# Attention values one unit later, and five input and two memory weight chunks in products of rounded parts, in a fused transformer kernel on one Trainium2 core

## The reference

```python
h = _rmsnorm(x, norm_mix[l])
proj = h @ w_in[l]
(c_q, c_kv, k_rope, fq, fk, fv, f_logit, cq, ck, cv) = jnp.split(proj, IN_SPLIT_POINTS, axis=-1)
ya = _mla(c_q, c_kv, k_rope, ...)      # 4 heads, q and kv from low-rank latents
yb = _fox(fq, fk, fv, f_logit, ...)    # 4 heads, scores with a cumulative forget term
yc = _chunk_rel(cq, ck, cv, ...)       # 4 heads, banded, relative bias
...
k, v = jnp.split(m @ w_ckv, 2, axis=-1)   # _cross: keys and values of the normed memory
...
p = jax.nn.softmax(sc, axis=-1)
return jnp.einsum('bhqk,bkhd->bqhd', p, v)
```

## Time and profile before

| | |
|---|---|
| median of 3 runs | 2479.87 us (2477.61 to 2480.54) |
| the profiled execution | 2479.72 us |
| its span, first to last instruction | 2477.9 us |
| mean granted TensorE clock | 0.989 of full speed |
| TensorE busy, weight loads busy | 96%, 84% of the span |
| VectorE, ScalarE, GpSimd busy | 77%, 21%, 12% |
| start up to the first attention's scores | 0 to 102.0 us |
| first attention (scores to last values) | 102.0 to 157.1 us |
| second attention | 213.9 to 229.4 us |
| third attention | 1503.1 to 1548.2 us |

### The profile page before, as it was taken

How to read it: one execution, slowest core, us unless ns; L and a number is a source line. 1 busy time by engine, 2 the same in 40 slices (tenths; PEclk the granted TensorE clock), 3 DMA queues, 4 the chain that set the end, 5 groups by cost and what they waited for, 6 DMA issues and landing times.

```text
span 2477.9 us, 38599 instructions
## 1 busy us (share of the span) xinstructions
PE 2387.2 (96%) x14244; PEld 2069.3 (84%) x14244; DVE 1908.7 (77%) x3950; ACT 530.2 (21%) x956; POOL 298.0 (12%) x228
## 2 busy tenths in 40 slices
PE   8998999999999999999999997899999999999998
PEld 7765998669897899999999876598978999999997
DVE  2226787768998788888888775489987888888887
ACT  2324333222233200000000145222332000000001
POOL 0000000016581000000000000165810000000000
PEclk9989999999999999999999999999999999999999
DMA  6504688963314555555555551133145555555553
GB/s 223 192 32 166 244 315 324 363 256 129 102 52 145 179 185 187 186 186 186 186 186 186 189 201 50 68 136 101 46 150 173 186 186 186 186 186 186 186 186 127
DMA packets 97875, 430.07 MB, mean 174 GB/s; under 512 B 11249, under 2 KB 11889, under 8 KB 90865
## 3 DMA queue, kind: packets, MB, share of 16 engines
q1 hardware_dynamic: 97776, 428.75, 48.6%
HBM read 427.66 MB, written 1.05 MB: 173 GB/s over the span
## 4 chain that ended last, share of the span: by engine, by line
PE 84%; DVE 12%; ACT 2%; issue 1%; DMA 1%; SPq 0%; DVEq 0%; ACTq 0%; PEldq 0%
PE ps L497 64%; PE ps L538 7%; PE ps L757 4%; DVE HN L1753 4%; PE ps L551 4%; DVE HN L1751 3%; PE ps L588 1%; PE ps L609 1%; ACT arena L966 1%; DVE arena L1763 1%; PE ps L570 1%; PE ps L719 1%; ACT arena L996 1%; PE ps L783 1%; DVE ring_rounded L1771 0%
## 5 line engine op out<-in xcount | busy, mean ns | idle before, releaser
L497 PE MATMUL ps<-ring_rounded,HN_rounded 128*128 128x512 f32 x3072 | 743.7, 392 | 8.5 <-DVE ring_rounded L1771 4.8
L497 PEld LDWEIGHTS ps<-ring_rounded,HN_rounded 128*128 128x128 f32 x3072 | 561.7, 189 | 127.6 <-issue 14.9
L497 PE MATMUL ps<-ring_rounded 128*128 128x256 f32 x3264 | 619.4, 283 | 0.0
L1771 DVE TENSOR_TENSOR ring_rounded<-ring,ring_rounded 128x1024 fp32r<-128x1024 f32 x460 | 561.7, 1222 | 20.5 <-ACT ring_rounded L1184 13.5
L497 PEld LDWEIGHTS ps<-ring_rounded 128*128 128x128 f32 x3264 | 522.3, 191 | 7.9
L497 PE MATMUL ps<-HT_rounded,ring_rounded 128*128 128x256 f32 x1632 | 461.8, 283 | 0.0
L1767 DVE CAST ring_rounded<-ring 128x1024 fp32r<-128x1024 f32 x406 | 280.3, 690 | 155.3 <-DMA ring<-in_experts_u 153.1
L497 PEld LDWEIGHTS ps<-HT_rounded,ring_rounded 128*128 128x128 f32 x1632 | 312.5, 191 | 7.9
L1194 ACT ACTIVATE HN<-ps 128x256 f32<-128x256 f32 x204 | 78.5, 385 | 1062.0 <-PE ps L497 1062.0
L757 PE MATMUL ps<-HT,ring 128*128 128x256 f32 x832 | 202.2, 381 | 1.4 <-ACT arena L966 1.4
L2088 POOL TENSOR_TENSOR ring_rounded<-ring,parts 128x1024 fp32r<-128x1024 f32 x8 | 18.8, 2373 | 1404.0 <-ACT parts L1136 1404.0
(11 more groups left out here) (252 smaller groups left out, 2677.1 us busy)
## 6 DMA issues: line engine op xcount, KB each, us to landing
ring<-in_experts_u SPq DMA_DIRECT2D x256, 512.0 KB, 4.2
ring<-in_experts_v SPq DMA_DIRECT2D x256, 512.0 KB, 3.5
ring<-in_stream SPq DMA_DIRECT2D x45, 2048.0 KB, 8.6
arena<-in_ada SPq DMA_DIRECT2D x96, 512.0 KB, 7.1
ring<-in_stream SPq DMA_DIRECT2D x2, 1024.0 KB, 6.2
arena<-in_keys SPq DMA_DIRECT2D x2, 1024.0 KB, 13.3
ring<-in_stream SPq DMA_DIRECT2D x1, 1664.0 KB, 8.5
ring<-in_stream SPq DMA_DIRECT2D x1, 1040.0 KB, 19.6
```

The lines of the kernel that those rows point to most:

```text
L497: mm = pe.matmul(out_, p, q, start=(first and i == 0), stop=(last and i == 2))
L1771: return dve.tensor_tensor(dst, src, h.bitcast(F32), ALU.subtract)
```

## The change

It has two parts.

**Values one unit later.** In step i of an attention TensorE now does `turn_probs(i)`, `scores(i+2)`, `values(i-1)`; the last unit's values come after the loop. VectorE's `weigh` moves in the same way, and the maxima and sums get four buffers in place of three. Two groups of fillers, before the values of units 4 and 6, go; that before unit 15 stays.

**Parts.** `("win", 1..4)`, `("ck",)` and `("cv",)` join `IN_PARTS`. Their high parts are written by ScalarE into `start_high` (two buffers), the low parts by VectorE in the ring; the activations are split into `start_ht` (the normed input) and `mem_parts` (the memory). `win 0` keeps plain products. SyncE loads `win 1` ahead of the memory, and `c_row` later.

```diff
@@
-           "mix_1": 20, ("gu", 0): 6, ("probs", 0): 6, ("probs", 6): 6, ("probs", 8): 9, ("values", 4): 5, ("values", 6): 5, ("values", 15): 5}
+           "mix_1": 20, ("gu", 0): 6, ("probs", 0): 6, ("probs", 6): 6, ("probs", 8): 9, ("values", 15): 5}
-IN_PARTS = [("gu", i) for i in range(FT // 2)] + [("down", i) for i in range(6)] + [("od", i) for i in range(1, 6)]
+START_PARTS = [("win", i) for i in range(1, 5)] + [("ck",), ("cv",)]
+IN_PARTS = START_PARTS + [("gu", i) for i in range(FT // 2)] + [("down", i) for i in range(6)] + [("od", i) for i in range(1, 6)]
@@ TensorE, attention
                     turn_probs(u)
                     if i + 2 < len(units):
                         scores(units[i + 2])
-                    values(u)
+                    if i:
+                        values(units[i - 1])
+                values(units[-1])
@@ TensorE, start
             for i in range(5):
-                wait_weights(pe, ("win", i))
-                n = WIN[i + 1] - WIN[i]
-                w = r3(weights(("win", i)), KT)
-                (turned if i in (1, 3) else rows)(("win", i), ("win", i), HT, w, n, norm=None if i else "mix")
+                name = ("win", i)
+                if i == 0:
+                    wait_weights(pe, name)
+                    rows(name, name, HT, r3(weights(name), KT), WIN[1], norm="mix")
+                elif i in (1, 3):
+                    turned_in_parts(name, 0 if i == 1 else None, start_ht)
+                else:
+                    rows_in_parts(name, HT_PARTS["mix"], start_ht)
@@
-            wait_weights(pe, ("ck",))
-            turned(("ck",), "ck", mem_t, r3(weights(("ck",)), KT), 512, norm="mem")
+            pe.wait_ge(sem("ht_parts"), HT_PARTS["mem"])
+            turned_in_parts(("ck",), None, mem_parts, "ck")
@@
-            wait_weights(pe, ("cv",))
-            rows(("cv",), "cv", mem_t, r3(weights(("cv",)), KT), 512)
+            rows_in_parts(("cv",), HT_PARTS["mem"], mem_parts, "cv")
@@ VectorE, attention
-                    weigh(u)
-                    behind(i)
+                    if i:
+                        weigh(units[i - 1])
+                        behind(i - 1)
+                weigh(units[-1])
+                behind(len(units) - 1)
@@ SyncE
             load(0)
+            load(1)
             sp.dma_start(mem.rearrange("p b n -> p (b n)"), d["mem"]).then_inc(sem("mem_loaded"), 16)
-            load(1)
@@
-                if name == ("ck",):
-                    sp.wait_ge(sem("h_ready"), H_READY["mem"])
+                if name == ("wcq",):
+                    sp.wait_ge(sem("stored"), STORED["cv"])
```

More of the change, by code:

```diff
@@ L211, in program @@
         rtmp = r3(one.take(4 * 64), 4)
+        start_ht = [r3(a, KT) for a in (hn_r, parts_r[:, one.at - parts_at:one.at - parts_at + KT * T])]
         flb = one.take(2 * 4 * T).rearrange("p (b h k) -> p b h k", b=2, h=4)
         nfl = one.take(2 * 4 * P).rearrange("p (b h k) -> p b h k", b=2, h=4)
+        start_high = r3(parts_r[:, one.at - parts_at:one.at - parts_at + 2 * SLOT], 2)
         ymix = r3(one.take(2 * D), NB)
@@ L217, in program @@
         pt_buf = one.take(2 * D).rearrange("p (u m a q) -> p u m a q", u=2, m=4, a=2)
+        mem_parts = [r3(parts_r[:, one.at - parts_at + i * KT * T:one.at - parts_at + (i + 1) * KT * T], KT) for i in (1, 0)]
         mem_t = r3(one.take(KT * T), KT)
@@ L305, in program @@
         fz = r3(small[:, 2:34], 4).rearrange("p a (b h) -> p a b h", b=2)
-        mx = r3(sb("mx", 12)[:, :], 3)
-        sums = r3(sb("sums", 12)[:, :], 3)
+        mx = r3(sb("mx", 16)[:, :], 4)
+        sums = r3(sb("sums", 16)[:, :], 4)
         rinv = r3(small[:, 50:58], 2)
@@ L1017, in _ @@
             root("mix", arrived="x_loaded")
+            act.wait_ge(sem("consts"), 48)
+            high_part(("win", 1))
             act.wait_ge(sem("mem_loaded"), 16)
             root("mem")
-            act.wait_ge(sem("consts"), 48)
+            high_part(("win", 2))
             for b in range(NB):
@@ L1027, in _ @@
                 put(fqk[:, 2 * i:2 * i + 2].rearrange("p a t -> p (a t)"), (("win", 1), i))
+            high_part(("win", 3))
             for b in range(NB):
@@ L1030, in _ @@
             stored("pc")
+            high_part(("win", 4))
             for i in range(2):
                 put(cqk[:, 2 * i:2 * i + 2].rearrange("p a t -> p (a t)"), (("win", 3), i))
+            high_part(("ck",))
             for b in range(NB):
@@ L1249, in _ @@
             stored("g1_1")
-            attention(ATT["diff"], lambda i: sub_squares(0) if i == 4 else None)
+            attention(ATT["diff"], lambda i: sub_squares(0) if i == 5 else None)
             load_table(ACT.Sqrt)
@@ L1400, in weigh @@
                 dve.wait_ge(sem("probs"), u["no"] + 1)
-                step(dve.reciprocal(rinv[:, k, :], sums[:, u["no"] % 3, :]))
+                step(dve.reciprocal(rinv[:, k, :], sums[:, u["no"] % 4, :]))
                 settle()
@@ L1482, in _ @@
             gain("mix", HT, col("norm_mix"))
+            split_ht(HT, start_ht)
+            low_part(("win", 1))
+            scale("mem")
+            low_part(("win", 2))
+            scale("lat")
+            lat_g = cols[:, COLS["q_norm"][0]:COLS["q_norm"][0] + 3]
+            gain("lat", lat_t, lat_g, nk=3)
+            low_part(("win", 3))
+            gain("mem", mem_t, col("norm_mem"))
+            low_part(("win", 4))
+            split_ht(mem_t, mem_parts)
             dve.wait_ge(sem("masks"), 64)
@@ L1499, in _ @@
             dve.sem_inc(sem("forget_in"), 1)
+            low_part(("ck",))
+            low_part(("cv",))
             dve.wait_ge(sem("stored"), STORED["mla"])
```

53 lines of the change are left out of this document (27 added, 26 removed).

## The result

The changed kernel takes **2461.65 us** (median of 4 runs, 2461.13 to 2464.41), the kernel before beside it 2478.74 (2477.25 to 2480.54): a ratio of 0.9933, 95% interval 0.992 to 0.9945, 17.1 us less. Run again later it took 2461.06 (2457.34 to 2464.20) against 2478.40, ratio 0.9926 (0.9913 to 0.994). The forecast was 2459.3. Its profiled execution took 2461.26 us, with a span of 2459.5, against 2479.72 and 2477.9. One thing on the title: it counts five input chunks, but four go in parts, `win 1` to `win 4`; `win 0` stays plain.

A forecast was written before the change was run, and what follows sets the result against it. Gains had to come from the start, bound by TensorE, and three attentions, limited by instruction order. 3.6 + 5.1 + 1.8 + 10.0 = 20.5 us off gave 2459.3 us, range 2453.5 to 2468.

The forecast's parts named there:

- The price of the products: Start products in parts on TensorE: 11.4 us per turned chunk against 13.81, together 12.1 us saved if nothing waits.
- The start: Input chunks, `ck` and `cv` in parts: 3.6 us gained after a pause ahead of `ck`, between 0.5 and 6.
- The first attention: Six units, values one unit later: 10 us gained, about half of it clock, between 4 and 10.5.
- The second attention: Two units, second values no longer wait behind transposes and copy: 1.8 us gained, with little room.
- The third attention: Eight units, values one unit later, about 4.0 us a unit in place of 4.93: 5.1 us gained, between 3.5 and 7.
- Rest: Everything outside start and attentions: buffers and `c_row` cost nothing, and behind each stage the work only shifts.
- four signs of being wrong: `ck` after 74, a wait ahead of the heads' transposes, six-unit stage over 50 us, third-attention values still every 4.9.
- A: Half clock stays in the first attention, half of its 10 us is lost: 2464.3 us; chance 0.20.
- C: Everything at its better end, no clock loss at the pause: 2454 us; chance 0.08.
- D: Attention scores still wait for VectorE; third stage gains 2 us, first 5: 2467 us; chance 0.07.
- B: The start gains nothing: `ck` lands 1 us later, rotation comes last, clock costs double: 2463 us; chance 0.09.
- E: Slower: clock falls in the pause before `ck` and stays at half through the first attention: 2495 us; chance 0.02.

The follow-up runs named there:

- win_only: The changed kernel with only the four input chunks in parts, `ck` and `cv` plain products: 2455.21 us, ratio 0.991 to the kernel before.
- ck_plain: The changed kernel with `ck` plain, `cv` in parts behind the `mla` stores and the rotation, the memory split later: 2453.34 us, ratio 0.9894 to the kernel before.
- parts_only: The changed kernel with the old order of the attentions, fillers back, so only the start is in parts: 2473.94 us, ratio 0.9983 to the kernel before.

## Why the prediction was right, point by point

- **The price of the products.** 11.4 us were forecast for a turned chunk, 5.8 for `win 2`, 5.7 for `win 4` and 11.2 for `cv`. It came to 11.5 for `win 1` and `win 3`, 11.3 for `ck` at full clock, some 5.8, 5.7 and 11.2. The row's 0.233 us for 512 columns held: `cv`'s 48 products took 11.19.
- **The start**, forecast 3.6 us, got 2.5 (1.7 in the second profile). The layout was right in each step: `win 1` at 24.45 (24.7 forecast), `win 3` at 44.66 (44.9), `ck` behind a pause that ends with its low part. Two terms were too small. The load of `ck` took 8.55 us where 7.9 stood, so `ck` began at 72.97, not 72.3. And the clock's price was 2.3 us (13.64 against 11.31 with the pause filled) where 1.7 was taken, from a wait of 2.2 us: a pause more than twice as long cost a third more, and 3.0 in the second profile (14.30).
- What the prediction wrote down and did not follow up: nearly all that the four input chunks win is lost to `ck`'s chain. By its own numbers a plain `ck` at 67.2 would have ended at 81.0, before the one in parts (83.7). `win_only` and `ck_plain` show it.
- **The first attention**, forecast 10, got 9.5, and is 45.6 us long (45 forecast). The laid-out split, 4.8 by the order and some 5 by the clock, was measured as 5.1 and 4.4. The reason given for the clock, the wait of 1.51 us, is only half right: `parts_only` had the wait without the dip. The 4.4 us are what the profiled execution of before paid, not a constant of its order: that they came as laid out is in part luck.
- **The second attention**, forecast 1.8 "with little room", got 0.8, and 1.9 in the second profile. The difference is the lower clock: 1.94 us for transposes where 1.07 was due, 4.20 for the values where 3.81 was. Six more profiles of the new order with these waits have 13.5 us as well, so 1.9 is the usual gain and 0.8 the exception. The room was the clock's.
- **The third attention**, forecast 5.1, got 4.2. The steps are 3.92 us (4.0 forecast). The bounding was named as what would show near the end, and a wait of 2.01 us did; the squares behind it on ScalarE, which held the last exponentials as long, were not named. Not in the sum was that this wait brings a dip: 1.4 us. With both moved, the stage takes 37.7. The layout itself was short for both orders, 43.4 for 45.1 and 38.3 for 40.9; the forecast used the difference, in which most of that cancels.
- **Rest.** "Behind each stage the work only shifts" was wrong in the small: `wcq` and `wco` lost 1.7 us each, transposes and `odo` won 0.9 and 1.5. On the whole these places add 1.4 us to the terms' 17.0 in the profiled execution, and nothing in the medians. One minus the granted clock, summed over the windows up to 2400, is 23.8 us before and 23.9 after: the clock that the first attention won back was lost again, at `ck`, around the second attention, near 440 and in the third.
- **The sum.** Each of the four terms came out smaller than forecast, by 0.5 to 1.1 us, 17.0 in place of 20.5. So the forecast was a little hopeful throughout, and the medians (17.1 and 17.3 us) agree with the smaller sum. None of the four signs of being wrong came.
- The rivals: A did not come, C neither (the start gave 2.5 of its 6 us and the third attention 4.2 of its 7), nor D (the period is 3.92). B came half: the clock cost more and the start gave 2.5 or 1.7. E did not: full clock was back by 78, 5 us into `ck`.

## What to carry to other kernels

Before a product is made cheaper by preparing its operand, lay out when the operand can be ready: a chunk whose load starts late is better left plain, and the same treatment pays on the next chunk, whose preparation is covered. In a loop over three engines, putting a consumer one unit later removes the wait for the copy, and then whatever stands once in the loop becomes a wait (here 1.6 us of bounding on VectorE ahead of the last soft, and the squares that follow it on ScalarE ahead of the last exponentials). Look for it on each engine and move it behind the last producer. When two profiles are compared, ask first how far apart they are where the edit begins: here it was up to 5 us. And a gain that comes from the clock in one profile should be checked in a second one, or with the waits filled, before it is counted.

## What the runs showed of the hardware

Identical waits of TensorE (1.51 us ahead of values, 1.38 and 0.79 ahead of `wcq`, 1.01 ahead of `wco`) were followed by full clock in some profiles and by the lower one (1.2 in place of 2.4 GHz) in others: `wcq` took 15.75 us in 4 of 12 profiles and 14.07 in 8. Behind the pause of 5.9 us ahead of `ck` the dip was always there: window 70 to 80 at 0.66 to 0.69 in all six profiles that have it open, `ck` at 12.85 to 14.30 us, and gone in the one with the pause filled. In stages that the change leaves alone, a wait of 3.42 us (near 1407 in the changed kernel, 1419 before) had the dip behind it in all fourteen profiles, and one of 2.96 us (ahead of the third attention) in five of them. The Trainium skill (TensorE: Matmul & The Clock Gate, section Why this matters for your kernels) says that a long enough idle gap between bursts sends the clock back. Behind the 5.9 and 3.42 us these traces agree each time. They also show the dip behind gaps of 0.8 to 1.9 us, but only sometimes; it then cost 0.9 to 1.7 us at the products named here, and 4.4 us in the first attention of before, where it lasted over 10 us.
